# Six input tiles of one layer as products of halves, in a kernel for two transformer blocks

## The reference

```
h = modulate(x, g_norm1, sh1, sc1);  hc = modulate(xc, g_norm1, ...)
proj = h @ w_in;  projc = hc @ w_in            # layer 0: all columns for both
c_kv, k_rope, k_g, v_g = split(proj[..., :KV_COLS])
c_q (384 columns), q_g (8 heads x 64 = 512)    # low-rank queries, grouped queries
f (512)                                        # input of the Fourier mix
q_gqa = rms_norm(q_g per head) with g_qn_gqa, then rope
o_four = real(fftn(f over tokens and over the 128 of a group))
q_mla = rms_norm(rms_norm(c_q, g_cq) @ w_uq);  kv = rms_norm(c_kv, g_ckv) @ w_ukv
```

## Time and profile before

| what | value |
|---|---|
| median of 3 runs | 2502.84 us (2501.11 to 2503.05) |
| profiled execution | 2505.26 us |
| its span | 2503.5 us |
| mean granted clock of TensorE | 0.998 |
| busy share PE / DVE / ACT / POOL | 98 / 53 / 22 / 25% |
| HBM read | 331.72 MB, 133 GB/s over the span |

### The profile page before, as it was taken

How to read it: one execution, slowest core, us unless ns; L and a number is a source line. 1 busy time by engine, 2 the same in 40 slices (tenths; PEclk the granted TensorE clock), 3 DMA queues, 4 the chain that set the end, 5 groups by cost and what they waited for, 6 DMA issues and landing times.

```text
span 2503.5 us, 37953 instructions
## 1 busy us (share of the span) xinstructions
PE 2453.6 (98%) x14528; PEld 2024.2 (81%) x14528; DVE 1335.4 (53%) x2707; ACT 548.7 (22%) x1199; POOL 621.4 (25%) x536
## 2 busy tenths in 40 slices
PE   9999999999999999999999999999999999999999
PEld 6757889996799999645567767888888875899999
DVE  6676467741325776324836763545542247435775
ACT  2132122111212221214620002222200215212220
POOL 1101135420212544001012221333241010232543
PEclk9999999999999999999999999999999999999999
DMA  8745344433333453120024662121222120243453
GB/s 313 284 186 201 127 162 153 193 131 135 117 135 119 168 193 135 66 87 26 2 84 156 218 260 88 68 101 71 110 93 80 68 95 26 104 166 153 168 193 110
DMA packets 39128, 334.67 MB, mean 134 GB/s; under 512 B 3920, under 2 KB 9168, under 8 KB 21712
## 3 DMA queue, kind: packets, MB, share of 16 engines
q1 hardware_dynamic: 32080, 307.61, 33.0%
q0 software_dynamic: 6912, 25.17, 2.7%
HBM read 331.72 MB, written 1.05 MB: 133 GB/s over the span
## 4 chain that ended last, share of the span: by engine, by line
PE 89%; DVE 5%; DMA 3%; issue 2%; ACT 1%; POOL 1%; SPq 0%; DVEq 0%; POOLq 0%; ACTq 0%
PE PS L767 25%; PE PS L569 15%; PE PS L1016 11%; PE PS L2799 6%; PE PS L1583 4%; PE PS L1743 4%; PE PS L2840 4%; PE PS L1728 3%; PE PS L2318 2%; PE PS L1384 2%; PE PS L1372 1%; DMA arena<-in_mod 1%; PE PS L436 1%; DMA slot<-in_weights 1%; PE PS L748 1%
## 5 line engine op out<-in xcount | busy, mean ns | idle before, releaser
L569 PE MATMUL PS<-XN,slot 128*128 128x256 f32 (+1 forms) x1184 | 296.8, 411 | 0.8 <-DVE XN L508 0.8
L767 PE MATMUL PS<-SQ,slot 128*128 128x128 f32 (+1 forms) x1984 | 294.4, 301 | 1.8 <-DVE slot L859 1.8
L569 PEld LDWEIGHTS PS<-XN,slot 128*128 128x128 f32 x1184 | 224.4, 190 | 69.8 <-issue 42.5
L767 PEld LDWEIGHTS PS<-SQ,slot 128*128 128x128 f32 x1984 | 268.1, 191 | 14.9 <-DVE slot L859 2.0
L1016 PE MATMUL PS<-arena,slot 128*128 128x128 f32 (+1 forms) x1902 | 251.5, 293 | 3.7 <-DVE arena L1094 2.2
L767 PE MATMUL PS<-XN,slot 128*128 128x128 f32 (+1 forms) x1664 | 250.0, 301 | 0.0
L1016 PEld LDWEIGHTS PS<-arena,slot 128*128 128x128 f32 x1902 | 239.1, 192 | 13.5 <-DVE arena L1094 2.8
L767 PEld LDWEIGHTS PS<-XN,slot 128*128 128x128 f32 x1664 | 226.1, 192 | 10.7
L886 DVE SCALAR_TENSOR_TENSOR arena<-PS,small,arena 128x255 f32<-128x255 f32 (+2 forms) x352 | 174.8, 544 | 44.7 <-ACT arena L830 44.1
L830 ACT ACTIVATE arena<-PS,small 128x256 f32<-128x256 f32 (+1 forms) x176 | 105.3, 617 | 399.3 <-DVE PS L919 238.9
L612 DVE CUSTOM_DVE_ANT_0 arena<-arena 128x1024 f32<-128x1024 f32 x80 | 107.3, 1382 | 30.2 <-DMA arena<-in_mod 30.2
(11 more groups left out here) (302 smaller groups left out, 3828.2 us busy)
## 6 DMA issues: line engine op xcount, KB each, us to landing
slot<-in_weights SPq DMA_DIRECT2D x85, 2048.0 KB, 7.8
slot<-in_weights SPq DMA_DIRECT2D x16, 2816.0 KB, 9.7
slot<-in_weights SPq DMA_DIRECT2D x24, 1536.0 KB, 6.8
arena<-in_mod POOLq DMA_DIRECT2D x48, 512.0 KB, 6.5
arena<-in_mod SPq DMA_DIRECT2D x48, 512.0 KB, 3.3
slot<-in_weights SPq DMA_DIRECT2D x5, 1024.0 KB, 5.5
slot<-in_weights SPq DMA_DIRECT2D x2, 2176.0 KB, 8.4
arena<-in_c SPq DMA_DIRECT2D x2, 1024.0 KB, 12.0
```

What stands on the lines that cost most here:

```text
L569: mm = pe.matmul(o, l, r, start=k == 0, stop=k == len(terms) - 1, skip_group_check=True)
L767: mm = pe.matmul(PS[:, bank, 0:h], lhs[:, k * P:(k + 1) * P], rhs(k), start=first and k == 0, stop=last and k == 3, skip_group_check=True)
```

## The change

The last six of the eleven query tiles are made in three pairs: `q_g` 2 and 3, `f` 0 and 1, `f` 2 and 3. The weights of a pair form a block matrix A with four quarters (output tile by even or odd k), the tokens a block matrix B (even or odd k by tokens or context). Seven products of 4 matmuls over 256 columns and sums replace the eight products. Sums of tokens t1 to t4 are made once by VectorE into free space (TQ), between the two norms; sums of weights s1, s3 per pair by GpSimd and s2, s4 by VectorE, in the slab's own slot (each pair has a slab of 32 tiles, with room for sums behind them); sums of results u2, u3, c22, c21, c12 by VectorE, from PSUM. c22 and c21 go to `Q_C2`, the upper tile stays in PSUM. The stage that was four slabs of 32 is two of 32, one of 16 and three pair slabs of 32. Layer 1 is as before.

```diff
--- before.py
+++ after.py
@@ -82,11 +82,17 @@
     st += ffn_stages("a1", "ffn_w_up1", "ffn_w_down1")
     for l in range(2):
         w = f"w_in_2{l}"
-        st.append((f"kvq{l}", cut(
-            down_tiles(w, DK, range(2)) + down_tiles(f"w_kr{l}", DK, [0])
-            + down_tiles(w, DK, [0], col=288)
-            + down_tiles(w, DK, [0], col=416) + down_tiles(w, DK, range(3), col=544)
-            + down_tiles(w, DK, range(4), col=928) + down_tiles(w, DK, range(4), col=1440))))
+        first = down_tiles(w, DK, range(2)) + down_tiles(f"w_kr{l}", DK, [0]) + down_tiles(w, DK, [0], col=288)
+        first += down_tiles(w, DK, [0], col=416) + down_tiles(w, DK, range(3), col=544)
+        if l == 0:
+            st.append(("kvq0", cut(first + down_tiles(w, DK, range(2), col=928))))
+            pairs = []
+            for col, m in ((928, 2), (1440, 0), (1440, 2)):
+                q0, q1 = [down_tiles(w, DK, [m + i], col=col) for i in range(2)]
+                pairs.append(q0[0::2] + q0[1::2] + q1[0::2] + q1[1::2])
+            st.append(("pairs0", pairs))
+        else:
+            st.append(("kvq1", cut(first + down_tiles(w, DK, range(4), col=928) + down_tiles(w, DK, range(4), col=1440))))
         ukv = []
         ukv += down_tiles(f"w_ukv_k{l}", 2, range(4))
         ukv += down_tiles(f"w_uq_n{l}", 3, range(4)) + down_tiles(f"w_uq_r{l}", 3, range(2))
@@ -2364,7 +2370,133 @@
                     dst = CQ[:, j, :]
                     return [("scalar", act_op(dst, PS[:, bank, :]))] if j % 2 else \
                         [("vector", copy_op(dst, PS[:, bank, :]))]
-                jobs = feature_jobs(xq, lambda k: None, 11, q_reads, segs=qseg)
+                jobs = feature_jobs(xq, lambda k: None, 5, q_reads, segs=qseg)
+                Q_PAIRS = 3
+                TQ = area(0, 16 * T).rearrange("p (s k t) -> p s k t", s=4, t=T)
+                Q_P1, Q_U2, Q_U3 = [area(4096 + T * i, T) for i in range(3)]
+                Q_C2 = [spare[0][:, i, :] for i in range(2)]
+
...
+                def pair_reads(i, s=s, l=l):
+                    upper = q_reads(5 + 2 * i, i % 2)
+                    j, src = 6 + 2 * i, Q_C2[i % 2]
+                    if j >= 7:
+                        lower = fold_reads(s, j, FR[:, j - 7, :].rearrange("p (g t) -> p g t", t=T),
+                                           src.rearrange("p (g t) -> p g t", t=T))
+                    else:
+                        lower = query_reads(j, QG[:, j - 3, :], SQ_GQ[(j - 3) // 2][:, (j - 3) % 2, :], src, l)
+                    return upper, lower
+
+                def vector_token_sums(dve, s=s):
+                    b11, b12, b21, b22 = [XQ[:, :, e, g * T:(g + 1) * T] for e in range(2) for g in range(2)]
+                    t1, t2, t3, t4 = [TQ[:, j] for j in range(4)]
...
+                    dve.tensor_tensor(t1, b12, b11, ALU.subtract).then_inc(*tick(VD, s, "t1"))
+                    dve.tensor_tensor(t3, b22, b12, ALU.subtract).then_inc(*tick(VD, s, "t3"))
+                    dve.wait_ge(*of(s, "t1"))
+                    dve.tensor_tensor(t2, b22, t1, ALU.subtract).then_inc(*tick(VD, s, "t2"))
+                    dve.wait_ge(*of(s, "t2"))
+                    dve.tensor_tensor(t4, t2, b21, ALU.subtract).then_inc(*tick(VD, s, "t4"))
+
+                def vector_pair_sums(dve, i, s=s):
+                    slot, _, _ = pair_slot(i)
+                    a11, a12, _, _ = [slot[:, 4 * j * P:(4 * j + 4) * P] for j in range(4)]
+                    s1, s2, s4 = [slot[:, (16 + 4 * j) * P:(20 + 4 * j) * P] for j in range(3)]
+                    dve.wait_ge(*of(s, "s3", i))
+                    dve.tensor_tensor(s2, s1, a11, ALU.subtract).then_inc(*tick(VD, s, "s2", i))
+                    dve.wait_ge(*of(s, "s2", i))
+                    dve.tensor_tensor(s4, a12, s2, ALU.subtract).then_inc(*tick(VD, s, "sums", i))
+
+                def gpsimd_query_pairs(pool, s=s):
+                    for i in range(Q_PAIRS):
+                        slot, sem, landed = pair_slot(i)
+                        a11, _, a21, a22 = [slot[:, 4 * j * P:(4 * j + 4) * P] for j in range(4)]
+                        pool.wait_ge(sem, landed)
+                        pool.tensor_tensor(slot[:, 16 * P:20 * P], a21, a22, ALU.add).then_inc(*tick(GD, s, "s1", i))
+                        pool.tensor_tensor(a21, a11, a21, ALU.subtract).then_inc(*tick(GD, s, "s3", i))
+
+                def tensor_query_pairs(pe, s=s):
...
+                    for i in range(Q_PAIRS):
+                        slot, sem, landed = pair_slot(i)
+                        a11, a12, s3, a22 = [slot[:, 4 * j * P:(4 * j + 4) * P] for j in range(4)]
+                        s1, s2, s4 = [slot[:, (16 + 4 * j) * P:(20 + 4 * j) * P] for j in range(3)]
+                        ba, bd = i % 2, 2 + i % 2
+                        pe.wait_ge(sem, landed)
+                        claim(pe, ba)
+                        product(a11, XQ[:, :, 0, 0:T], ba, last=False).then_inc(*tick(TD, s, "p1", i))
+                        pe.wait_ge(*of(s, "sums", i))
+                        if i == 0:
+                            pe.wait_ge(*of(s, "t4"))
+                        claim(pe, 4)
+                        product(s2, TQ[:, 1], 4).then_inc(*tick(TD, s, "p6", i))
+                        claim(pe, 5)
+                        product(s3, TQ[:, 2], 5).then_inc(*tick(TD, s, "p7", i))
+                        claim(pe, bd)
+                        product(s1, TQ[:, 0], bd, last=False).then_inc(*tick(TD, s, "p5", i))
+                        claim(pe, 7)
+                        product(a22, TQ[:, 3], 7).then_inc(*tick(TD, s, "p4", i))
+                        pe.wait_ge(*of(s, "p1_copied", i))
+                        product(a12, XQ[:, :, 1, 0:T], ba, first=False)
+                        pe.wait_ge(*of(s, "c22", i))
+                        product(s4, XQ[:, :, 1, T:2 * T], bd, first=False)\
+                            .then_inc(*tick(TD, "slab", first_slab["pairs0"] + i))
...
+                        upper, _ = pair_reads(i)
+                        lend(ba, (s, "c12", i), *[(s, "read", 5 + 2 * i, r) for r in range(len(upper))])
+                        lend(bd, (s, "c12", i))
+                        lend(4, (s, "u2", i))
...
+                def scalar_query_pair(act, i, s=s):
+                    if i < Q_PAIRS:
+                        act.wait_ge(*of(s, "p1", i))
+                        if i:
+                            act.wait_ge(*of(s, "u2", i - 1))
+                        act.activation(Q_P1, PS[:, i % 2, 0:T], ACT.Copy).then_inc(*tick(SD, s, "p1_copied", i))
+                    if i:
+                        for part, made in zip((1, 0), ("c21", "c12")):
+                            act.wait_ge(*of(s, made, i - 1))
+                            _, op = pair_reads(i - 1)[part][0]
+                            op(act).then_inc(*tick(SD, s, "read", 5 + 2 * (i - 1) + part, 0))
+
+                def vector_query_pair(dve, i, s=s):
+                    bd = 2 + i % 2
+                    dve.wait_ge(*of(s, "p6", i))
+                    dve.wait_ge(*of(s, "p1_copied", i))
+                    dve.tensor_tensor(Q_U2, PS[:, 4, 0:T], Q_P1, ALU.add).then_inc(*tick(VD, s, "u2", i))
+                    dve.wait_ge(*of(s, "u2", i))
+                    dve.wait_ge(*of(s, "p7", i))
+                    dve.tensor_tensor(Q_U3, PS[:, 5, 0:T], Q_U2, ALU.add).then_inc(*tick(VD, s, "u3", i))
+                    dve.wait_ge(*of(s, "u3", i))
+                    dve.wait_ge(*of(s, "p5", i))
+                    if i >= 2:
+                        dve.wait_ge(*of(s, "read", 6 + 2 * (i - 2), 0))
+                    dve.tensor_tensor(Q_C2[i % 2][:, T:2 * T], PS[:, bd, 0:T], Q_U3, ALU.add).then_inc(*tick(VD, s, "c22", i))
+                    dve.wait_ge(*of(s, "p4", i))
+                    dve.tensor_tensor(Q_C2[i % 2][:, 0:T], Q_U3, PS[:, 7, 0:T], ALU.subtract).then_inc(*tick(VD, s, "c21", i))
+                    if i < Q_PAIRS - 1:
+                        vector_pair_sums(dve, i + 1)
+                    dve.wait_ge(*of(s, "p3", i))
+                    dve.tensor_tensor(PS[:, i % 2, T:2 * T], PS[:, bd, 0:T], Q_U2, ALU.add).then_inc(*tick(VD, s, "c12", i))
+                    for part, made in zip((1, 0), ("c21", "c12")):
+                        dve.wait_ge(*of(s, made, i))
+                        for r, (_, op) in list(enumerate(pair_reads(i)[part]))[1:]:
+                            op(dve).then_inc(*tick(VD, s, "read", 5 + 2 * i + part, r))
             else:
                 jobs = []
                 for j in range(6):
@@ -2421,6 +2553,8 @@
                 scale=1.0 / 256, eps="plain", ring=2, ready=[[(f"kv{l}", "read", 1, 0)]],
                 jobs[0])
+            if l == 0:
+                add(vector=vector_token_sums)
             add_linear(s, jobs[:cq_jobs])
             add(gpsimd=lambda p, cos=gpsimd_cos, done=gpsimd_done, m=rope_m, t=kr_tmp: (cos(p, "KRAW", KRAW, m[1]),
```

(35 more changed lines are left out.)

## The result

The changed kernel takes 2508.52 us in the median of 20 runs against 2502.95 in the median of 20 of before. The ratio is 1.0023, with a 95% interval of 1.0014 to 1.0033: slower by 5.8 us (3.5 to 8.3), where 2505.2 and no measurable change were forecast. Measured again later, the ratio was 1.0012 (1.0001 to 1.0023), 3.0 us. Before, it is 1125.48 − 1070.55 = 54.93 us (its start and the middle of it are in the earlier trace rows).

What follows compares the result with a forecast made beforehand. TensorE, busy 98% of the span, was taken as the bound. Saving 4.93 us, waits of 3.06 and 2.01 and a clock fall of 2.3 gave +2.4 us: 2505.2 us in the median, range 2501.3 to 2508.6.

Steps and rivals of the forecast that it cites:

- The sum at full clock: Changed stage without clock loss: 4.93 us saved, waits of 3.06 and 2.01 us added, +0.14 us in all.
- The two waits: TensorE waits for bank 0 at the first pair, 3.06 us, and at the start of the low-rank stage, 2.01 us.
- The clock at the first wait: Behind the idle at the first pair the clock falls, costing between 1.6 and 3.05 us, taken as 2.3.
- The row at 190 us: Earlier trace: idles of 0.87 and 1.24 us ahead of 188.80 and 191.14 lowered the clock, losing 1.6 us.
- The row at 328 us: Earlier trace: TensorE's longest idle, 2.79 us before 328.14, with the clock at 0.50 behind it, losing 3.05 us.
- the clock at the second wait: Behind the 2.0 us idle ahead of the low-rank stage the clock was forecast to stay full, at no cost.
- Rival B: Clock falls at both waits, each costing 1.6 to 3.05 us: 2506.1 to 2509.0 us, chance 0.25.
- The weights of a pair: Loads land in 7.5 us and weight sums end before TensorE needs them, thinnest slack 2.4 us at pair 2; no cost.
- rival D: Waits held hidden are not: late weight sums in a pair or late token sums; +3.3 to +7 us, chance 0.08.
- The sums of tokens: Four VectorE sums between key norm and copy of tile 0, 1.22 us each, hide in 5.86 us of idle.
- The contention of GpSimd and VectorE: Weight sums on both engines slow one another through shared SBUF interfaces, at most 0.9 us at pair 2.
- The rule of the clock gate: Throttled is TensorE's default and activity releases it, so a long idle brings the lower clock; without it, +0.1 us.

Runs made afterwards that it cites:

- the waits filled: Changed kernel with six throwaway matmuls ahead of the first pair's claim of bank 0 and four ahead of the low-rank stage's: ratio 1.0004 to before, stage 55.53 us.
- the version without waits: Changed kernel with pairs beginning in banks 1 and 3, pair 0's VectorE weight sums ahead of the query norm, low-rank banks 0, 2, 1, 3: ratios 0.9982, 0.9994, 0.9981.

## Why the prediction was wrong

- **The sum at full clock** was right. The two waits were given as 3.06 and 2.01 us; from start to start they are 3.17 and 2.20, ended by the instructions named. What was too small is the way from the last read to TensorE, taken as 0.04 us and measured as 0.14 and 0.26. A pair takes 12.09, the saving is 4.93. That sum said +0.14; with the waits filled and the clock at 1.00 it is +0.60, of which 0.3 are those two ways and 0.15 the slower first product behind each idle (1.80 and 6.94 us instead of 1.73 and 6.86).
- **The clock at the first wait** was right in kind and too high in size: I took 2.3, the middle of 1.6 and 3.05. It fell in 7 of 8 profiles with an idle of 3.0 us there, and cost 1.7 to 1.8 each time. The row at 190 us was the near one. The row at 328 us was one execution: in the changed kernel's trace the same work stands at 327.02 behind 2.66 us of idle, at a mean clock of 0.76 over 6.98 us, which loses 1.7 us and not 3.05. The upper price was not a property of that idle either.
- **The step that failed is the clock at the second wait**: "I leave it at full clock in the forecast." It fell in 5 of 7 profiles with an idle of 2.05 us, the changed kernel's first among them, at 1.7 to 1.8 us. So a term put at nothing was 1.78. An idle of 1.81 that kept the clock was one execution of one idle, and I read it as a property of the length. (In five other profiles that idle was 1.28 to 1.61 us and kept it as well.) Rival B, both falls, was the case, with 0.25; its sum of 0.1 + 3.2 = +3.3 at the lower price is the 3.98 of the trace within 0.7. The median measured, 2508.52, lies near the upper end of B's range, but not for B's reason: no fall in this stage cost the upper price. Taking the falls at these shares, the sum would have been 0.14 + 0.9 x 1.8 + 0.7 x 1.8 = +3.0.
- **The weights of a pair** were mis-sized. A pair slab has 16 tiles and 1024 KB, not the 32 and 2048 told ahead of the prediction. They land in 4.7 us, not 7.5. This hardly changed the cover, since the load was not what came last: VectorE's sums for pair 1 start at 1087.30, right behind c21, and end at 1088.71, 3.2 us ahead of their use at 1091.94, as the prediction had it. For pair 2 they end at 1100.80, again 3.2 us ahead (1104.03), where 2.4 were given. No product inside a pair of the changed kernel waited, and rival D had no ground there.

```profile
slot<-in_weights SPq DMA_DIRECT2D x2, 1024.0 KB, 4.7
...
1087.30 0.69 DVE L2411 TENSOR_TENSOR slot<-slot 128x512 f32<-128x512 f32 x1
1088.02 0.69 DVE L2413 TENSOR_TENSOR slot<-slot 128x512 f32<-128x512 f32 x1
```

- **The sums of tokens** hid, as said, though with less room: the first took 1.66 us, the other three 1.21 to 1.23, and VectorE had 0.75 us left ahead of the copy of tile 2. The first is the one that ran beside a sum on GpSimd, in all 14 profiles of kernels with pairs.

```profile
1050.27 0.86 POOL L2533 TENSOR_TENSOR arena<-arena,small 128x256 f32<-128x256 f32 x1 [43.80 <-PE PS L2528]
...
1050.55 1.66 DVE L2399 TENSOR_TENSOR arena<-XN 128x1024 f32<-128x1024 f32 x1
1052.13 1.21 DVE L2400 TENSOR_TENSOR arena<-XN 128x1024 f32<-128x1024 f32 x1
...
1057.09 0.69 DVE L1564 COPY arena<-PS 128x512 f32<-128x512 f32 x1 [0.75 <-PE PS L575]
```

- **The contention of GpSimd and VectorE**, for which "GPSIMD Engine Reference" of the Trainium skill, section Specifications, was drawn on, did not touch the pairs: GpSimd's sums took 1.26 and 1.27 us there. VectorE was idle beside those of pairs 0 and 1 and had two sums of 0.42 us from PSUM beside those of pair 2. The 1.66 us above agree with that section, though no run moves one of the two sums, so it is not shown that GpSimd is the cause. No wait of TensorE came of it.
- **The rule of the clock gate** ("TensorE: Matmul & The Clock Gate" of the Trainium skill, section "What's actually happening": activity releases the throttle) agrees with the filled waits, 1.00 where 0.53 and 0.64 stood, and with the version without waits, 1.00 throughout. I had it as speaking against the change and then gave it one of the two idles.

## What to carry to other kernels

Where one engine is the bound and a saving is a few us, look first at which buffer each new piece claims and who reads it last: here two bank numbers cost 5.4 us of waits, and the clock another 3.5, against 4.9 saved; behind the first of them a misplaced pair of sums would have kept 2.5 us of idle even so. Price an idle like these (2 to 3 us on TensorE, in dense work) as itself and the fall behind it, by a chance and not by whether one such idle kept the clock. After freeing one thing behind a late engine, look at what else stands in the same queue.

## What the runs showed of the hardware

- One idle of one length, in the same program and place, keeps the granted clock in one execution (1.00 behind 3.01 us) and loses it in the next (0.55). The share was 7 of 8 at 3.0 us and 5 of 7 at 2.05; the one idle of 2.52 us lost it. The idle in the merge stage lost it in 7 of the 10 profiles where it was 2.0 us or more, one of 2.01 among them, and kept it at 2.52, 2.92 and 3.09. What decides it no run here shows.
- A fall in this stage cost 1.7 us, by profiles of the same kernel with and without it (58.91 and 57.21, 55.86 and 54.18, 54.91 and 53.22).
- Matmuls whose results nobody reads hold the clock as well as others: 2.6 and 1.7 us of them went with a stage shorter by 3.4 us, in one profile.
- The whole time of one kernel spreads over some 10 us between executions (before: 2498.47 to 2509.10 in 20 runs), while the stage repeats to 0.02 us where the clocks agree. A change of 0.2% is better read from the stage.
